# The first norm's modulation in four quarters instead of four halves, in a two-block transformer kernel

## The reference, cut to what matters

```python
cond = jax.nn.silu(c)                                    # 1024 numbers
mod = (cond @ ada_w[0] + ada_b[0])[:, None, :]           # 6 x 1024
sh1, sc1, g1, sh2, sc2, g2 = jnp.split(mod, 6, axis=-1)
h = rmsnorm(x, norm1_g[0]) * (1 + sc1) + sh1             # 256 x 1024
proj = h @ w_in + b_in                                   # the mixer's projections
...
```

## Time and profile before

| | |
|---|---|
| median of three runs | 1455.65 us (1454.43 to 1456.05) |
| the profiled execution | 1453.79 us, of which its span 1452.0 us |
| PE busy | 1430.3 us, 99% of the span |
| ACT, DVE, POOL busy | 756.5, 722.8, 1211.7 us |
| DMA read | 310.87 MB, 215 GB/s over the span |

### The profile page before, as it was taken

The page is one execution under the profiler, slowest core; times in us unless marked ns, Lnnn a source line. Parts: engine busy times, 40 slices in busy tenths (PEclk is TensorE's granted clock), DMA queues, the critical chain, the costliest instruction groups (busy, mean ns, idle before and its releaser), DMA issues.

```text
span 1452.0 us, 21556 instructions
## 1 busy us (share of the span) xinstructions
PE 1430.3 (99%) x7600; PEld 1199.9 (83%) x7600; DVE 722.8 (50%) x1556; ACT 756.5 (52%) x1275; POOL 1211.7 (83%) x986
## 2 busy tenths in 40 slices
PE   7999999999999999999999999999999999999997
PEld 5898777799988987778888888878888888788886
DVE  7863654766643754754566303454650044655202
ACT  4435775644445345765644445574654345655442
POOL 3899989898888987559898897967999977789995
PEclk9999999999999999999999999999999999999999
DMA  9994557688975986337676565643656656446651
GB/s 361 402 357 159 192 170 227 232 305 314 315 263 161 399 314 219 110 102 232 216 244 205 185 206 164 191 154 131 191 201 196 221 163 188 132 163 200 195 199 56
DMA packets 149559, 313.35 MB, mean 216 GB/s; under 512 B 10934, under 2 KB 31818, under 8 KB 149451
## 3 DMA queue, kind: packets, MB, share of 16 engines
q1 hardware_dynamic: 147696, 310.62, 63.6%
q10 hardware_dynamic: 1756, 1.35, 0.3%
HBM read 310.87 MB, written 1.06 MB: 215 GB/s over the span
## 4 chain that ended last, share of the span: by engine, by line
PE 92%; DVE 4%; ACT 2%; POOL 1%; DMA 1%; issue 1%; SPq 0%; POOLq 0%; DVEq 0%; ACTq 0%
PE bank L814 58%; PE bank L859 12%; PE bank L860 8%; PE bank L857 5%; PE bank L1022 1%; PE bank L1006 1%; POOL lo_units L751 1%; PE bank L895 1%; PE bank L992 1%; DMA x_rows<-in_x 1%; PE bank L1109 1%; PE bank L1038 1%; PE bank L1074 1%; ACT hi_units L1402 1%; PE bank L1064 0%
## 5 line engine op out<-in xcount | busy, mean ns | idle before, releaser
L751 POOL TENSOR_TENSOR lo_units<-raw_units,hi_units 128x512 fp32r<-128x512 f32 (+3 forms) x928 | 1151.5, 1276 | 219.2 <-ACT hi_units L1402 218.0
L1402 ACT ACTIVATE hi_units<-raw_units 128x1024 fp32r<-128x1024 f32 (+1 forms) x470 | 482.7, 1030 | 410.9 <-PE bank L814 248.4
L814 PE MATMUL bank<-hi_units,turned 128*128 128x512 f32 (+3 forms) x1600 | 441.2, 390 | 1.7 <-DVE turned L1940 0.8
L814 PEld LDWEIGHTS bank<-hi_units,turned 128*128 128x128 f32 x1600 | 291.6, 189 | 53.3 <-DVE turned L1940 2.8
L860 PE MATMUL bank<-turned,lo_units 128*128 128x256 f32 x1024 | 288.0, 281 | 0.0
L814 PE MATMUL bank<-hi_units,turned_wide 128*128 128x512 f32 x992 | 274.6, 391 | 0.0
L859 PE MATMUL bank<-turned,hi_units 128*128 128x512 f32 x736 | 259.2, 397 | 0.0
L814 PE MATMUL bank<-lo_units,turned 128*128 128x512 f32 (+3 forms) x800 | 252.7, 383 | 0.8 <-POOL lo_units L751 0.5
L814 PEld LDWEIGHTS bank<-hi_units,turned_wide 128*128 128x128 f32 x992 | 185.3, 188 | 38.5 <-issue 0.5
L860 PEld LDWEIGHTS bank<-turned,lo_units 128*128 128x128 f32 x1024 | 194.3, 190 | 0.2
L814 PEld LDWEIGHTS bank<-lo_units,turned 128*128 128x128 f32 x800 | 149.7, 188 | 30.6 <-POOL lo_units L751 3.6
(11 more groups left out here) (266 smaller groups left out, 1290.9 us busy)
## 6 DMA issues: line engine op xcount, KB each, us to landing
ada_units<-in_ada_w SPq DMA_DIRECT2D x88, 512.0 KB, 7.7
raw_units<-in_w_ffn_tiles SPq DMA_DIRECT2D x72, 512.0 KB, 5.5
raw_units<-in_mlp_w_out SPq DMA_DIRECT2D x64, 512.0 KB, 3.3
raw_units<-in_mlp_w_tiles SPq DMA_DIRECT2D x56, 512.0 KB, 3.3
raw_units<-in_w_in SPq DMA_DIRECT2D x56, 458.0 KB, 9.8
raw_units<-in_w_in SPq DMA_DIRECT2D x48, 512.0 KB, 6.8
raw_units<-in_w_ffn_out SPq DMA_DIRECT2D x44, 512.0 KB, 3.5
raw_units<-in_moba_w_qkv SPq DMA_DIRECT2D x24, 512.0 KB, 3.7
```

Source lines behind the costliest of these rows:

```text
L751: pool.tensor_tensor(LO[:, s, b, 0:w], RAW[:, u["slot"], b, 0:w], HI_[:, s, b, 0:w].bitcast(F32), ALU.subtract).then_inc(lo_ready.sem, lo_ ...
L814: ins = pe.matmul(BANK[2 * c["pair"] + t][:, 0:w], (A[a] if A is BT else A[:, a])[:, part, t * P:(t + 1) * P], W[:, s, b, 0:w], start=(i = ...
L1402: act.activation(HI_[:, s, 0:n, 0:w], RAW[:, u["slot"], 0:n, 0:w], ACT.Copy)\
```

## The change

The four chunks are no longer halves of scale and shift but *quarters*: quarter q is 256 columns of the scale beside 256 columns of the shift, put side by side in a new input (`ada_first`), in which the 4 KB that a unit needs for a partition lie together. A quarter thus serves exactly one group of two k-tiles, and one unit each of c0 and c1. Biases and gain come as ready columns (`first_columns`). The loads of c and of the constants go to ACT's queue; x is loaded behind two units instead of five. The work on PE, ACT and DVE becomes a loop over quarters.

```diff
-    scale0, shift0, scale1, shift1 = first = [ada(0, c) for c in (2, 0, 3, 1)]
+    first = [ada(0, q) for q in range(N_FIRST)]
-    stream.extend(scale0["units"] + shift0["units"])
+    sums = [u for c in first for u in c["units"]]
...
+            behind = {4: (c0, 0), 5: (c1, 0), 8: (c0, 1), 9: (c1, 1), 12: (c0, 2), 13: (c1, 2)}
+            for n, u in enumerate(sums):
+                stream.append(u)
+                if n in behind:
+                    c, i = behind[n]
+                    stream.append(c["units"][i])
+            stream.extend((c0["units"][3], c1["units"][3], vec(*vec0), vec(*vec1)))
...
-        sp.dma_start(COND, dram["c"].rearrange("b (p k) -> (b p) k", p=P)).then_inc(c_in, 16)
-        sp.dma_start(CON[:, 0:n_early], dram["constants"][:, 0:n_early]).then_inc(const_in, 16)
...
-                if (l, c, i) == (0, 0, 1):
+                if (l, c, i) == (0, 0, 2):
                     for t in range(NT):
                         sp.dma_start(X[:, t, :], dram["x"][0, t * P:(t + 1) * P, :]).then_inc(x_in[t], 16)
...
+        def column_sums(q):
+
+            pe.wait_ge(ada_used.sem, ada_used.at(quarters[q]["units"][-1]["index"]))
             for j in range(4):
+                ins = pe.matmul(columns[:, 4 * q + j:4 * q + j + 1], MOD[:, q * CW + j * P:q * CW + (j + 1) * P], ONES[:, 0:1],
+                                start=j == 0, stop=j == 3)
+            ins.then_inc(product.sem, product.mark(("columns", q)))
...
+        keep_running(4, BANK[3])
...
                 turn(tag, O, range(4), 0, ready)
                 turn(tag, O, range(4), 1, ready)
+                keep_running(1, BANK[3])
+                column_sums(0)
+                keep_running(1, BANK[3])
+                for q in range(N_FIRST):
+                    pe.wait_ge(turned_lo.sem, turned_lo.at((tag, q)))
+                    unit(c0, q, HT)
+                    if q + 2 < N_FIRST:
+                        turn(tag, O, range(4), q + 2, ready)
+                    unit(c1, q, HT)
+                    if q + 1 < N_FIRST:
+                        column_sums(q + 1)
...
+        def first_hi(q):
+
+            act.wait_ge(rows.sem, rows.at(("columns", q)))
+            act.wait_ge(turned.sem, turned.at((("n1", 0), q)))
+            bank = BANK[(TQ, TP)[q % 2]]
+            for k in (0, 1):
+                part = bank[:, k * S:(k + 1) * S]
+                ins = act.activation(part, part, ACT.Identity, scale=GAINED[:, 2 * q + k:2 * q + k + 1], bias=BIASED[:, 4 * q + 2 + k:4 * q + 3 + k])
+            ins.then_inc(act_side.sem, act_side.mark(("whole", q)))
+            act.wait_ge(act_side.sem, act_side.at(("whole", q)))
+            act.activation(HT[:, 2 * q:2 * q + 2, 0, :], bank[:, :].rearrange("p (k s) -> p k s", k=2), ACT.Copy)\
+                .then_inc(turned_hi.sem, turned_hi.mark((("n1", 0), q)))
...
-        prep(2)
...
+                for q in range(N_FIRST):
+                    if q == N_FIRST - 1:
+                        prep(2 * q + 1)
+                    first_hi(q)
+                    prep(2 * q + 2)
...
+        def first_columns(q):
+
+            dve.wait_ge(first_in, 16)
+            dve.wait_ge(product.sem, product.at(("columns", q)))
+            cols = slice(4 * q, 4 * q + 4)
+            link(v.tensor_tensor(BIASED[:, cols], BANK[SB_[1]][:, cols], FIRST_BIAS[:, cols], ALU.add))
+            say(v.scalar_tensor_tensor(GAINED[:, 2 * q:2 * q + 2], BIASED[:, 4 * q:4 * q + 2], 1.0, FIRST_GAIN[:, 2 * q:2 * q + 2], ALU.add, ALU.mult),
+                ("columns", q))
...
+                for q in range(N_FIRST):
+                    more = q + 1 < N_FIRST
+                    if more:
+                        first_sum(q + 1, 0)
+                    first_columns(q)
+                    if more:
+                        first_sum(q + 1, 1)
+                        first_sum(q + 1, 2)
+                    turn_lo(("n1", 0), HT, part=slice(q, q + 1))
+                    if more:
+                        for kt in range(3, KT):
+                            first_sum(q + 1, kt)
```

More of the change, by code:

```diff
@@ L91 @@
 NPR, NU = 7, 3
-FIRST_BANK = {(0, 2): 0, (0, 0): 0, (0, 3): 0, (0, 1): 0}
-PE_UNITS = {(0, 3, 1)}
+N_FIRST = 4
+FIRST_BANK = {(0, q): 0 for q in range(N_FIRST)}
 ADA_HOME = (("gates",) * 8 + ("mod",) * 2 + ("masks",) * 2, ("masks",) * 6 + ("gates",) * 4 + ("masks",) * 2)
@@ L1212, in column_products @@
[L1212 to L1232, removed]
@@ L1234, in keep_running @@
-        def keep_running(n):
-            for _ in range(n):
-                pe.matmul(BANK[3][:, :], con("ident"), ada_raw(scale0["units"][0])[:, 0, :], start=True, stop=True)
-        pe.wait_ge(ada_in[scale0["units"][0]["home"]][scale0["units"][0]["slot"]], 16)
-        keep_running(1)
-        pe.wait_ge(first_gain_in, 16)
-        gain_columns(0)
-        pe.wait_ge(first_bias_in, 16)
-        bias_columns(scale0)
-        keep_running(2)
-        column_sums(scale0)
+        quarters = [todo.pop(0) for _ in range(N_FIRST)]
@@ new lines, in column_sums, with keep_running @@
+        def column_sums(q):
+            pe.wait_ge(ada_used.sem, ada_used.at(quarters[q]["units"][-1]["index"]))
+            for j in range(4):
+                ins = pe.matmul(columns[:, 4 * q + j:4 * q + j + 1], MOD[:, q * CW + j * P:q * CW + (j + 1) * P], ONES[:, 0:1],
+                                start=j == 0, stop=j == 3)
+            ins.then_inc(product.sem, product.mark(("columns", q)))
+        def keep_running(n, bank):
+            for _ in range(n):
+                pe.matmul(bank[:, :], con("ident"), ada_raw(quarters[0]["units"][0])[:, 0, :], start=True, stop=True)
@@ L1247, in _ @@
+        first_unit = quarters[0]["units"][0]
+        pe.wait_ge(ada_in[first_unit["home"]][first_unit["slot"]], 16)
+        keep_running(4, BANK[3])
         for l in range(DEPTH):
@@ L1698, in _ @@
                       allow_slow_non_contiguous=True).then_inc(pos_in, 16)
-        act.wait_ge(c_in, 16)
-        act.activation(CT, COND, ACT.Tanh, scale=0.5).then_inc(act_side.sem, act_side.mark("cond"))
-        act.dma_start(GAIN_ROW, dram["norm1_g"][0:1, :]).then_inc(first_gain_in, 16)
-        act.wait_ge(cleared.sem, cleared.at("second shift"))
-        act.wait_ge(rows.sem, rows.at("cleared"))
-        act.dma_start(FIRST[0:1, :], dram["ada_b"][0:1, 0:4 * CW]).then_inc(first_bias_in, 16)
         act.wait_ge(const_in, 16)
@@ L1878, in ada_upto @@
                 raw = ada_raw(u)
-                mine = [i for i in range(KT // UNIT_K) if (u["l"], u["c"], i) not in PE_UNITS]
                 partial = BANK[SB_[by_key["ada", u["l"], u["c"]]["bank"]]][:, :]
@@ L1890, in ada_upto @@
                         continue
-                    total = MOD[:, cols] if (u["i"], k) == (mine[-1], UNIT_K - 1) and not in_two(u["l"], u["c"]) else partial
+                    total = MOD[:, cols] if kt == KT - 1 and not in_two(u["l"], u["c"]) else partial
                     ins = v.scalar_tensor_tensor(total, raw[:, k, :], COND[:, kt:kt + 1], partial, ALU.mult, ALU.add)
@@ L2618, in in_tiles, with in_quarters @@
     return out
+def in_quarters(inputs):
+    w, b, g = (np.asarray(inputs[name])[0] for name in ("ada_w", "ada_b", "norm1_g"))
+    half = CW // 2
+    cols = [np.concatenate([np.arange(D + q * half, D + (q + 1) * half), np.arange(q * half, (q + 1) * half)]) for q in range(N_FIRST)]
+    first = np.stack([w[:, c].reshape(P, KT, CW) for c in cols])
+    columns = np.concatenate([b[c].reshape(4, P) for c in cols] + [g.reshape(KT, P)]).T
+    return {"in_ada_first": np.ascontiguousarray(first), "in_first_columns": np.ascontiguousarray(columns)}
 def kernel(**inputs):
```

123 lines of the change are left out of this document (34 added, 89 removed).

## The result

The changed kernel took 1461.87 us (median of five runs, 1459.69 to 1462.66) against 1455.65 for the kernel before: a ratio of 1.0038, 95% interval 1.0026 to 1.0050. It is 6.2 us slower; the forecast was 4.3 slower, 1460.0. The profiled execution is the one of 1461.87, with a span of 1460.1.

The account below looks back on a forecast made before the run. The prediction took PE to bound the kernel (92% of the chain), so that only the opening's end mattered: +1.8 us for tables and angles plus 2.5 for the clock, +4.3 on the median 1455.65, rounded to 1460.0; range 1456.0 to 1463.0.

Parts of the forecast that it names:

- first column sum starts: Opening on PE: quarter 0's column sum begins at 14.05 us, 0.04 behind DVE's sums at 14.0.
- three cycles at full clock: PE, from first to last column sum: cycles of 10.1, 10.1 and 9.65 us, without clock loss.
- the clock in them: Slow PE clock after three opening bubbles: 0.5 us for the first, 1.0 each for two bare ones, 2.5 together.
- last column sum to last low part done: End of the normed rows on DVE: last low part ends 4.0 us after the last column sum, at 47.9.
- tables and angles: DVE behind the last low part: fourteen small instructions done by 52.65 instead of 50.87 us, +1.8.
- angles to the third chunk's low part: Opening's end: behind the angles the same hi and lo unit follow as before; 2.70 us.
- handover: The forecast's bubble: from a column sum to the first matmul using its rows, 4.17 us in each quarter.
- part of a slow stretch falls into the waiting: Reason for pricing each bare bubble's clock loss at 1.0 us, nearer the measured 0.5 than the full 1.7.
- The rival of the full price: Every one of three opening bubbles pays 1.7 us of clock: +6.9 with the tables, 1462.6 us; chance 12%.
- nothing is added there: ACT's queue: taking c and the constants costs nothing, since two loads ahead of its tanh go behind it.
- covered by the tables: Fourth bubble, after the last column sum: no clock price counted, since DVE's tables cover it.
- No clock lost: Rival: PE keeps 2.4 GHz through bubbles of 3 us; +1.8, 1457.5 us; chance 20%.

Follow-up runs that it names:

- clock kept: Against the changed kernel: three products with zero weights added behind each column sum, three keep-running products in the first gap instead of one; 1457.45 us.
- tables early: Against the changed kernel: DVE's tables and angles moved from behind the last low part to its wait for the third quarter's column sum; 1462.03 us.
- a product a gap: Against the changed kernel: one zero-weight product added behind each of the three later column sums, first gap left as it was; 1461.16 us.
- c and the constants ahead: Against the changed kernel: loads of c and the constants put back on SP's queue ahead of the units; 1463.11 us.
- first handover covered: Against the changed kernel: next column sum ahead of c1's unit, three keep-running products behind the first column sum, none ahead; 1451.85 us, again 1451.35.

## Why the prediction came out 1.9 us low

| step | forecast | the changed kernel | difference |
|---|---|---|---|
| first column sum starts | 14.05 | 14.73 | +0.68 |
| three cycles at full clock | 29.85 | 29.60 (clock kept) | -0.25 |
| the clock in them | 2.5 | 4.57 | +2.07 |
| last column sum to last low part done | 4.0 | 3.88 | -0.12 |
| tables and angles | 4.75 | 4.92 | +0.17 |
| angles to the third chunk's low part | 2.70 | 2.75 | +0.05 |
| that low part starts | 57.87 | 60.45 | +2.6 |

The opening came 2.6 us later than forecast, the median only 1.9. The 6.88 us of the opening show as 6.2 between the medians and as 8.1 between the profiled executions (the step at 425 to 462 is in these); no run says why the medians show less, so that the miss is 1.9 and not 2.6 is luck as far as is known.

- **Direction and mechanism were right.** The delay is made in the opening and passes through one for one; PE's order sets it, with a handover of 4.1 us in front of each quarter; the units land ahead of their use throughout the opening.
- **The mis-sized term is the clock**: 2.5 us taken, 4.57 measured; by gap 0.5, 1.0 and 1.0 taken, 1.07, 2.32 and 1.18 measured. Two steps failed in it. The one that cost 0.75 us, in the first and the third gap, is "part of a slow stretch falls into the waiting". I had it from the earlier trace rows: in the kernel before the clock falls in 22 to 24 us, while PE is still at keep-running products, and c0's unit at 24.81 meets only the end of it. In the changed kernel the clock falls within 0.4 us of the units' start in these two gaps, so the slow stretch lies on units. The other 1.3 us were missed in the second gap. About 1 us of its slow stretch did fall into the waiting, and still it cost 2.32, more than the 1.7 that the prediction, going by the one slow stretch of the kernel before, had as the most for a gap: the clock stays below full there in four rows of 2 us in a row, where the others show three (18 to 24 us: 0.69, 0.50, 0.95; 42 to 48: 0.67, 0.50, 0.98). Which gap is long varies (the second in the changed kernel, in the one with tables early and in the one with a product a gap, the third, 11.77 us, with c and the constants ahead); what decides it stays open.
- **The rival of the full price** (1462.6, given 12%) was 0.7 us off, nearer than the forecast: 3 x 1.7 is 5.1 for the clock, against 4.57. The rule of the Trainium skill that I set beside it (TensorE: Matmul & The Clock Gate, "HAM oscillation — how this bites in real kernels"), that bursts parted by waits start slow each time, agrees with the trace: all four bursts began at 1.53 to 1.87 us for four products. That they fall back in the wait the trace does not show for the third gap, where the clock was 1.00 to its end and fell 0.4 us into the burst.
- **The first column sum** came 0.68 late, and not by what the prediction had set aside for its upper bound: the eight keep-running passes took 6.09 us, less than the 7 to 8 that it allowed. They began at 7.07 instead of 4.9, because c and the constants landed 2.7 and 3.5 us later than before (c at 5.16, the constants at 6.65). So "nothing is added there" for the loads on ACT's queue was wrong: PE's start is added. It is no loss against SP's queue, since x, which is next in need, gained about as much; DVE's sums were done at 14.10, as forecast (14.0).
- **The tables** took what was forecast. That their 1.8 us was the price of the end was half the truth: with the fourth gap's slow products, PE reaches the same point by itself, which the prediction had left uncounted as "covered by the tables".
- **No clock lost** (20%, 1457.5) is refuted for this kernel and fits the kernel with the clock kept, 1457.45.

## What to carry to other kernels

A chain of hops from PE and back to it was dear twice here, once as idling and once at half clock behind it; ask first for independent products that can be put between the sum and its use, as c1's unit here, which turned +6.2 us into -2.0. A little cover may buy nothing: one product in a handover of 4 us changed next to nothing, three kept the clock. And when two things reach an end together, moving one of them alone shows nothing of its worth: the tables gave 0.2 us in one order and 0.6 in another.

## What the runs showed of the hardware that I had not expected

- In the changed kernel the granted clock stayed at 1.00 through a gap without any product (40 to 42 us) and fell when work had begun again (0.67 and 0.50 in the next two rows). After idle times of 0.47 to 1.21 us in the kernels with the clock kept and with the first handover covered, the next four products took 1.06 to 1.10 us; after 2.12 to 3.15 us in the changed kernel and in the one with a product a gap, they took 1.53 to 1.89. With c and the constants ahead they took only 1.24 and 1.14 after 2.19 and 3.00 us; there the clock fell later, inside the unit (0.50 from 20 us and 0.52 from 54 us on, in rows of 2 us).
- Products with a weight of zeros kept the clock in the second experiment: 1.00 from 16 to 60 us.
- The two loads on ACT's queue, issued at 0.72 and 1.17 us, landed at 5.16 and 6.65 although c is 4 KB, each 0.18 us behind a unit of 512 KB on SP's queue (4.98 and 6.47). On SP's queue, ahead of the units, they landed at 2.31 and 3.48.
